# Attention's queries and keys written in two rounded parts by the scan, and its 66- and 67-row products filled up to 128 rows with zeros

## The chip, the cores and the metric

The kernel runs on one core of a Trainium2 chip. The metric is the time of one execution on the device in microseconds, as the median of several runs; a profile describes one further execution. The engines are called as the profile calls them: PE (TensorE, matrix products) with PEld (its weight loads), DVE (VectorE), ACT (ScalarE), POOL (GpSimd) and SP (SyncE, which here only issues transfers).

## What is computed

Two layers of a sequence model, 2048 tokens by 1024 features in float32. Each layer multiplies the normalised input by one wide matrix, gives the columns to four groups (forgetting attention, RWKV-7 time mixing, sliding-window attention, a short convolution), gates the results and multiplies them by an output matrix. The change touches the first group, four heads of width 64:

```python
q = _rmsnorm(q, q_norm)
k = _rmsnorm(k, k_norm)
log_f = jax.nn.log_sigmoid((f_logit + b_f).astype(jnp.float32))
Ft = jnp.cumsum(log_f, axis=1).transpose(0, 2, 1)
s = jnp.einsum("bqhd,bkhd->bhqk", qi, k) * scale
s = s + Fi[..., :, None] - Ft[:, :, None, :]
s = jnp.where(kpos[None, :] <= qpos[:, None], s, -jnp.inf)
p = jax.nn.softmax(s, axis=-1)
out = jnp.einsum("bhqk,bkhd->bqhd", p, v)
```

## The kernel before

A layer runs five stages one behind the other: `phase_project` and `phase_rwkv_prep` (0 to about 430 us in the first layer), `phase_rwkv_scan` (to about 1050), `phase_fox` (1054 to about 1337) and `phase_swa_out`. The second layer repeats them 1594.5 us later. Each engine has its own program, written by hand, and semaphores order them.

**The scan.** `phase_rwkv_scan` runs over 16 tiles `t` of 128 tokens, about 38 us each. PE interleaves the recurrence's small products with the input projection's dense ones, which are dealt out by `fill(stage)`; so PE has work at nearly every point, but its program is in order. Beside this, 56 units of 128 rows by 256 tokens are normalised: 32 are the queries and keys of `phase_fox` (`turned(u)` is false), 24 belong to the sliding window (true: they are also rotated, on POOL). A tile from `t = 4` on has four units, the outer two turned, the inner two plain. A unit goes: SP loads `qx` (L696); ACT squares it into `qr` (`square`, L1098); PE sums (`norm_sum`, L916); ACT makes the factor (L1105, L1107); POOL scales (`scale`, L814, and L824 for the last product) and raises `q_out`; SP stores it into `projT` (`store_norm`, L711). There are two `qr` buffers, so `square` of unit `u` waits until POOL has raised `q_out` for unit `u - 2`. In tiles 4 to 14 POOL computes, ahead of unit `(t, 1)`, the low part of the projection's next weights (L115) and the gates' bias (L829). `square(t, 3)` waits for unit `(t, 1)`, and PE's `norm_sum(t, 3)` waits for `square(t, 3)`.

**The attention.** `phase_fox` works in rounds `R`: pairs of heads `p` = 0 and 1, by blocks `Q` of 512 queries (8 rounds). Queries and keys are used as sums of two rounded parts (type fp32r), high and low. There are two sorts of score product. The `s` steps (L1510) compute scores from the high parts alone, `Q2` by `K2`, over 66 rows (64 and two rows of ones against the forget terms); DVE takes their maxima (`fx_nm`, L1599), from which the subtrahend of a round is made and put into rows 64 to 66 of `Q2` (steps `x` and `l`, L1519 on PE, L1663 on ACT). The `m` steps compute the scores that are used: `K1` by `Q1` (L1534, 128 rows) and `K2` by `Q2` over 67 rows (L1535); ACT takes the exponential (L1680), PE multiplies by the values (L1487), DVE and POOL add up the denominators (L1581, L1465). `plan()` writes the order of all steps by hand: the `s` steps of round R + 1 run between the `m` steps of round R. Steps `v` turn a block of values (L1497, copied by DVE at L1594).

`Q1` is the low part of q over its high part, `K1` the high part of k over its low part, `K2` and `Q2` the high parts in rows 0 to 63. Before, these come from raw q and k (SP, L1405 and L1406, 7 transfers a block with the forget terms, L1407, and the values, L1410) by steps `r`: ACT rounds (L1651, L1652, L1657), DVE subtracts (L1588, L1589), POOL copies (L1453), for each of 8 blocks a layer. At the start POOL writes ones into three rows of `Q2` (L1444), for which PE, ACT and the first block wait.

Of the kernel before, what the change touches and what calls it, by code (L numbers as in the profile page):

```python
# [13 lines left out]
F32 = mybir.dt.float32  # L14
# [571 lines left out]
def phase_rwkv_scan(nc, l, rw, pend, par, consts, masks, rope, fa, mixT, projT, J):  # L586
# [10 lines left out]
    with ExitStack() as ctx:  # L597
# [27 lines left out]
        cs = P.sb("cs", [128, 2, UB])  # L625
        qr = [P.sb(f"qr{e}", [128, UB]) for e in two]
# [15 lines left out]
        def turned(u):  # L642
            return norms[u][0] > 3

# [44 lines left out]
        def _(sp):  # L689

            def load_norm(u):
                e, (r, b) = u % 3, norms[u]
                row, cols = row_of[r], slice(PAD + b * UB, PAD + (b + 1) * UB)
                if u > 2:
                    sp.wait_ge(q_st[e], 16 * (u // 3))
# [12 lines left out]
            def store_norm(u):  # L708
                e, (r, b) = u % 3, norms[u]
                sp.wait_ge(s["q_out"], u + 1)  # L710
                sp.dma_start(projT[row_of[r]:row_of[r] + 128, PAD + b * UB:PAD + (b + 1) * UB], qx[e][:]).then_inc(q_st[e], 16)  # L711
# [90 lines left out]
            for q in range(3):  # L802
                sp.wait_ge(q_st[q], 16 * ((NU - q + 2) // 3))
# [4 lines left out]
        def _(pool):  # L808
            G = nc.gpsimd

            def scale(u):
# [447 lines left out]
def phase_fox(nc, l, projT, fa, consts, mixT, E):  # L1259
# [6 lines left out]
    with ExitStack() as ctx:  # L1266
# [9 lines left out]
        rq, rk, rv = [rows[0:HD, h] for h in two], [rows[0:HD, 2 + h] for h in two], rows[:, 4]  # L1276
        high, low = (w[:].rearrange("p k c -> p (k c)") for w in (E.wo_hi, E.wo_lo))
        Q1, K1 = ([[high[:, (i + h) * T:(i + h + 1) * T] for h in two], [P.sb(f"{n}1{h}", [128, T], F32R) for h in two]] for n, i in (("qa", 0), ("ka", 2)))
        Q2, K2 = ([[low[0:KX, (i + h) * T:(i + h + 1) * T] for h in two], [P.sb(f"{n}1{h}", [KX, T], F32R) for h in two]] for n, i in (("qb", 0), ("kb", 2)))
# [5 lines left out]
        LS = P.sb("LS", [128, QT, KX])  # L1285
        rl = P.sb("rl", [128, TB])
# [4 lines left out]
        names = ("c_in", "c_rdy", "a_split", "k_split", "d_split", "p_split", "s_rdy", "m_rdy", "x_rdy",  # L1291
                 "lt_rdy", "lt_free", "l_rdy", "v_rdy", "t_rdy", "p_rdy", "pv_done", "add_d", "add_p", "rl_rdy", "o_free", "rl_free", "yo_rdy", "whi_rdy", "wlo_rdy", "th_rdy", "gate_d")
        s = {n: P.sem(n) for n in names}
        raw_in, v_in, yo_st = ([P.sem(f"{n}{b}") for b in two] for n in ("raw_in", "v_in", "yo_st"))
# [12 lines left out]
        def plan():  # L1307
# [835 lines left out]
```

## Time and profile before

| | |
|---|---|
| median of 3 runs | 3163.36 us (3154.23 to 3169.47) |
| the profiled execution | 3179.65 us |
| its span, first to last instruction | 3177.8 us |
| PE busy in the span | 2972.4 us (94%) |
| DVE, ACT, POOL busy | 1468.2, 1133.4, 979.7 us |
| mean granted clock of PE | 0.946 of full speed |

The profiled execution is 16.3 us above the median of the runs, and 1.9 us of it lie outside the span. Sums over the trace are made against 3179.65. "PEclk" is the clock that PE was granted, as a share of full speed: 1.00 is 2.4 GHz, 0.50 is 1.2 GHz. PE's busy time counts a product that runs at the low clock with its longer duration, so a full PE can still be slow.

### The profile page before, as it was taken

To read this page: it belongs to the slowest core of one execution; us is meant where nothing else is said; L and a number is where in the kernel's file an instruction comes from. 1 tells how busy PE (TensorE), PEld (TensorE's weight loads), DVE (VectorE), ACT (ScalarE), POOL (GpSimd) and SP (SyncE) were. 2 spreads that over 40 slices of the span, in tenths; PEclk is the share of its full clock that TensorE was granted. 3 is DMA by queue.
4 is the path that set the end of the run, shared out by engine and by line. 5 is a ranking of instruction groups with operands and counts; after the bars stand their busy time and mean duration, and the time that the engine had idled before them with its cause. 6 is when DMAs were issued, how large, how long until landed. Compare 5 with 4: busy or idle time off the path is not lost. (4 is left out here: it accounts for less than half of the span.)

```text
span 3177.8 us, 67901 instructions
## 1 busy us (share of the span) xinstructions
PE 2972.4 (94%) x26644; PEld 2180.4 (69%) x26644; DVE 1468.2 (46%) x2204; ACT 1133.4 (36%) x2284; POOL 979.7 (31%) x890
## 2 busy tenths in 40 slices
PE   7999989999999789889889999899999997999799
PEld 6867867777777444367668678677777775444577
DVE  5127733322222577567451277333222224766674
ACT  5004433333333344633250044333333333446332
POOL 5101112344444224532141011123444442236221
PEclk9999999999999679989989999999999996799899
DMA  5224543344443211266332245434444432112663
GB/s 153 77 75 154 165 115 97 111 120 125 121 122 104 68 37 40 74 197 203 127 119 76 75 154 162 116 92 116 121 120 118 123 108 71 37 38 64 199 202 110
DMA packets 421183, 358.01 MB, mean 113 GB/s; under 512 B 127624, under 2 KB 358280, under 8 KB 420872
## 3 DMA queue, kind: packets, MB, share of 16 engines
q1 hardware_dynamic: 350696, 320.14, 33.5%
q10 hardware_dynamic: 70176, 33.59, 4.1%
q8 instruction: 211, 3.46, 0.5%
q14 instruction: 100, 0.82, 0.1%
HBM read 222.84 MB, written 130.84 MB: 111 GB/s over the span
## 5 line engine op out<-in xcount | busy, mean ns | idle before, releaser
L129 PE MATMUL ch_acc<-h_hi,ch_w_hi 128*128 128x512 f32 (+1 forms) x2048 | 822.7, 402 | 21.2 <-PEq L126 20.4
L135 PE MATMUL ch_acc<-h_hi,ch_w_lo 128*128 128x512 f32 (+1 forms) x2048 | 828.5, 405 | 0.0
L133 PE MATMUL ch_acc<-h_lo,ch_w_hi 128*128 128x512 f32 (+1 forms) x2048 | 825.8, 403 | 0.2 <-issue 0.2
L129 PEld LDWEIGHTS ch_acc<-h_hi,ch_w_hi 128*128 128x128 f32 (+1 forms) x2048 | 381.7, 186 | 108.5 <-issue 24.0
L133 PEld LDWEIGHTS ch_acc<-h_lo,ch_w_hi 128*128 128x128 f32 (+1 forms) x2048 | 381.5, 186 | 98.1 <-issue 11.5
L135 PEld LDWEIGHTS ch_acc<-h_hi,ch_w_lo 128*128 128x128 f32 (+1 forms) x2048 | 380.6, 186 | 89.1 <-issue 0.3
L115 POOL TENSOR_TENSOR ch_w_lo<-ch_raw,ch_w_hi 128x1024 fp32r<-128x1024 f32 (+1 forms) x62 | 149.1, 2404 | 744.8 <-POOLq L114 744.8
L1680 ACT ACTIVATE fx_prob<-fx_ST 128x512 f32<-128x512 f32 (+3 forms) x320 | 156.2, 530 | 201.1 <-PE fx_ST L1535 96.3
L1927 PE MATMUL so_acc<-ea_wo_hi,so_m_hi 128*128 128x512 f32 x512 | 207.4, 405 | 6.8 <-POOL so_m_lo L1862 6.8
L1929 PE MATMUL so_acc<-ea_wo_lo,so_m_hi 128*128 128x512 f32 x512 | 203.7, 398 | 0.0
L1599 DVE TENSOR_REDUCE fx_nm<-fx_SS 128x2 f32<-128x1024 f32 (+3 forms) x160 | 167.6, 1060 | 76.5 <-PE fx_SS L1510 63.8
L814 POOL TENSOR_SCALAR rs_qx<-rs_qx,rs_gain 128x256 f32<-128x256 f32 x112 | 103.4, 924 | 322.1 <-ACT rs_qr L1098 305.8
L1928 PE MATMUL so_acc<-ea_wo_hi,so_m_lo 128*128 128x512 f32 x512 | 202.4, 395 | 0.0
L1465 POOL TENSOR_TENSOR fx_sump<-fx_sump,fx_prob 128x1024 f32<-128x1024 f32 (+2 forms) x60 | 130.0, 2166 | 214.0 <-ACT fx_prob L1680 213.0
L146 ACT COPY ch_stage<-ch_acc 128x512 f32<-128x512 f32 x192 | 112.3, 585 | 225.9 <-ACTq L145 225.8
L146 DVE COPY ch_stage<-ch_acc 128x512 f32<-128x512 f32 (+1 forms) x64 | 44.1, 689 | 260.6 <-DVEq L145 260.6
L1862 POOL TENSOR_TENSOR so_m_lo<-so_y,so_m_hi 128x512 fp32r<-128x512 f32 x64 | 87.5, 1368 | 246.2 <-ACT so_m_hi L1805 241.2
L110 ACT ACTIVATE ch_w_hi<-ch_raw 128x1024 fp32r<-128x1024 f32 x64 | 65.9, 1029 | 243.3 <-ACTq L109 243.3
L824 POOL TENSOR_TENSOR rs_qx<-rs_qx,rs_qr 128x256 f32<-128x256 f32 x112 | 82.0, 732 | 143.9 <-ACT rs_qr L1107 132.8
L1581 DVE TENSOR_TENSOR fx_sumd<-fx_sumd,fx_prob 128x1024 f32<-128x1024 f32 (+3 forms) x72 | 117.5, 1632 | 10.6 <-ACT fx_prob L1680 3.6
L1927 PEld LDWEIGHTS so_acc<-ea_wo_hi,so_m_hi 128*128 128x128 f32 x512 | 96.8, 189 | 32.8 <-POOL so_m_lo L1862 7.3
L1929 PEld LDWEIGHTS so_acc<-ea_wo_lo,so_m_hi 128*128 128x128 f32 x512 | 96.5, 189 | 23.3
(285 smaller groups left out, 4932.1 us busy)
## 6 DMA issues: line engine op xcount, KB each, us to landing
projT<-ch_stage SPq DMA_DIRECT2D x248, 256.0 KB
ch_raw<-w_in ACTq DMA_DIRECT2D x62, 512.0 KB, 5.5
pj_xb<-x SPq DMA_DIRECT2D x32, 512.0 KB, 4.6
so_stage<-x SPq DMA_DIRECT2D x64, 256.0 KB, 3.4
rp_pre<-projT SPq DMA_DIRECT2D x16, 899.5 KB, 7.7
rs_qx<-projT SPq DMA_DIRECT2D x112, 128.0 KB, 3.3
projT<-rs_qx SPq DMA_DIRECT2D x112, 128.0 KB, 1.8
rs_cs<-rope SPq DMA_DIRECT2D x48, 256.0 KB, 3.7
```

Source lines behind the costliest of these rows:

```text
L115: (G or self.nc.gpsimd).tensor_tensor(self.w_lo[q][:, :, 0:m], self.raw[:, :, 0:m], self.w_hi[q][:, :, 0:m].bitcast(F32), ALU.subtract).th ...
L129: ins = M(acc, self.w_hi[q][:, k, 0:m], self.h_hi[:, k, cols], start=(k == 0), stop=False)
L133: M(acc, self.w_hi[q][:, k, 0:m], self.h_lo[:, k, cols], start=False, stop=False)
L135: ins = M(acc, self.w_lo[q][:, k, 0:m], self.h_hi[:, k, cols], start=False, stop=(k == KC - 1))
L146: copy(self.stage[e][0:m, :], self.acc[e][0:m, :]).then_inc(self.stage_rdy[e], 1)
L1465: G.tensor_tensor(sump[R % 2][:, :, lo:TB], sump[R % 2][:, :, lo:TB], prob[nt % NP][:, :, lo:TB], ALU.add).then_inc(s["add_p"], 1)
L1581: V.tensor_tensor(sumd[R % 2][:, :, lo:TB], sumd[R % 2][:, :, lo:TB], prob[i % NP][:, :, lo:TB], ALU.add).then_inc(s["add_d"], 1)
L1599: V.tensor_reduce(nm[p][:, :, t, c:c + 1], SS[ns % 2][:, :, 0:width(t, c)], AX.X, ALU.max, negate=True).then_inc(s["m_rdy"], 1)
L1680: A(prob[nt % NP][:, h, lo:TB], ST[h][:, lo:TB], ACT.Exp).then_inc(s["p_rdy"], 1)
L1927: M(a, m_hi[e][:, c, rows], wo_hi[:, c, cols], start=(i == 0), stop=False)
L1928: M(a, m_lo[e][:, c, rows], wo_hi[:, c, cols], start=False, stop=False)
L1929: ins = M(a, m_hi[e][:, c, rows], wo_lo[:, c, cols], start=False, stop=(i == KC - 1))
```

## The change

In the scan, POOL makes for each of the 32 plain units a layer both rounded parts: the last product is written once as fp32r into a new buffer `qh` and once into `x`, and `x` less `qh`, rounded, is the low part. SP stores both into a new tensor `qk` (two transfers for one). In `phase_fox` the steps `r` go; SP loads the parts straight into `Q1`, `K1`, `Q2`, `K2`, now 15 transfers a block. `Q2` and `K2` have 128 rows; POOL writes ones and zeros into rows 64 to 127 first, block 0 ahead of the rest, and SP waits for that. `s` and `m` products read all 128 rows. The constants are loaded from ACT's queue.

```diff
 def scale(u):                                  # POOL, scan
                 pool.drain()
                 pool.wait_ge(s["q_fac"], u + 1)
+                if not turned(u):
+                    f = plain.index(u)
+                    if f > 1:
+                        pool.wait_ge(q_st[plain[f - 2] % 3], stores[plain[f - 2]])
+                    G.tensor_tensor(qh[f % 2][:], x[:], qr[u % 2][:], ALU.mult)
                 G.tensor_tensor(x[:], x[:], qr[u % 2][:], ALU.mult)
+                if not turned(u):
+                    pool.drain()
+                    G.tensor_tensor(x[:].bitcast(F32R), x[:], qh[f % 2][:].bitcast(F32), ALU.subtract)
                 pool.drain().then_inc(s["q_out"], 1)
...
 def store_norm(u):                             # SP, scan
+                    for part, buf in ((0, qh[plain.index(u) % 2][:].bitcast(F32)), (1, qx[e][:])):
+                        row = (r // 2 * 2 + part) * GW + r % 2 * 128
+                        sp.dma_start(qk[row:row + 128, b * UB:(b + 1) * UB], buf).then_inc(q_st[e], 16)
...
-            beside = [("r", 0, i) for i in range(4)] + [("v", 0, 0)]
-            splits = [(R, [("r", B, i) for B in bs for i in range(4)]) for R, bs in ((0, (1,)), (1, (2,)), (2, (3, 4)), (3, (5, 6, 7)))]
-            splits = dict(splits)
+            beside = []
+            splits = {R: [("v", B, 0) for B in bs] for R, bs in ((0, (0, 1)), (1, (2,)), (2, (3, 4)), (3, (5, 6, 7)))}
...
 # SP, phase_fox, for each block R
+                sp.wait_ge(s["zero_rdy"], 1 if R == 0 else 2 if R < NQ else 3)
                 for h in two:
-                    sp.dma_start(rq[h][:, R % 2], projT[R_FQ + r:R_FQ + r + HD, tok]).then_inc(raw_in[R % 2], 16)
-                    sp.dma_start(rk[h][:, R % 2], projT[R_FK + r:R_FK + r + HD, tok]).then_inc(raw_in[R % 2], 16)
-                    sp.dma_start(K2[p][h][HD:KX, cols].bitcast(F32), fa[...]).then_inc(raw_in[R % 2], 16)
+                    sp.dma_start(Q2[p][h][0:HD, cols].bitcast(F32), qh[rows_of[h]]).then_inc(a_in[R], 16)
+                    sp.dma_start(K2[p][h][0:HD, cols].bitcast(F32), kh[rows_of[h]]).then_inc(a_in[R], 16)
+                    sp.dma_start(K2[p][h][HD:KX, cols].bitcast(F32), fa[...]).then_inc(a_in[R], 16)
+                for h in two:
+                    for buf, lo, hi in ((Q1[p][h], ql, qh), (K1[p][h], kh, kl)):
+                        sp.dma_start(buf[0:HD, cols].bitcast(F32), lo[rows_of[h]]).then_inc(b_in[R], 16)
+                        sp.dma_start(buf[HD:128, cols].bitcast(F32), hi[rows_of[h]]).then_inc(b_in[R], 16)
...
 # POOL, phase_fox
+            def filled(part, c, p, a, n):
                 for h in two:
-                    G.tensor_copy(Q2[p][h][HD:KX, :], LS[HD:KX, 0, 0:1].to_broadcast([KX - HD, T]))
-            pool.drain().then_inc(s["c_rdy"], 1)
+                    G.tensor_copy(part[p][h][HD:128, a:a + n], fill[HD:128, c:c + 1].to_broadcast([128 - HD, n]))
+                pool.drain().then_inc(s["one_rdy" if c == 0 else "zero_rdy"], 1)
+            filled(K2, 1, 0, 0, TB)
+            filled(Q2, 0, 0, 0, TB)
+            filled(K2, 1, 0, TB, T - TB)
+            filled(Q2, 0, 0, TB, T - TB)
+            filled(K2, 1, 1, 0, T)
+            filled(Q2, 0, 1, 0, T)
...
 # PE, phase_fox
-                        ins = M(SS[ns % 2][:, h, 0:w], Q2[p][h][0:HD + 2, t * 128:(t + 1) * 128], K2[p][h][0:HD + 2, c * TB:c * TB + w], start=True, stop=(c < Q))
+                        ins = M(SS[ns % 2][:, h, 0:w], Q2[p][h][:, t * 128:(t + 1) * 128], K2[p][h][:, c * TB:c * TB + w], start=True, stop=(c < Q))
...
-                if k == "r" and x > 1:                     # DVE
-                    V.tensor_tensor(Q1[p][h][0:HD, c], rq[h][:, R % 2], Q2[p][h][0:HD, c].bitcast(F32), ALU.subtract)
-                    ins = V.tensor_tensor(K1[p][h][HD:128, c], rk[h][:, R % 2], K2[p][h][0:HD, c].bitcast(F32), ALU.subtract)
...
-                if k == "r" and x < 2:                     # ACT; x == 2: two copies more, POOL: two copies
-                    A(Q2[p][x][0:HD, c], rq[x][:, R % 2], ACT.Copy)
-                    ins = A(K2[p][x][0:HD, c], rk[x][:, R % 2], ACT.Copy)
```

## Rows read from the trace of the kernel before

**Rows 1.** Page: PE busy tenths and granted clock tenths in 40 equal slices.

```profile
PE   7999989999999789889889999899999997999799
...
PEclk9999999999999679989989999999999996799899
```

**Rows 2.** Windows: the scan stage of the first layer.

```profile
430.00:1050.00 620.00, 611.14 (x9226) 467.26 (x9224) 183.40 (x389) 214.45 (x552) 243.35 (x306) 0.99 0.39 111
```

**Rows 3.** Windows in phase_fox: us, busy (x) per engine, PEclk, DMA share, GB/s.

```profile
1080.00:1190.00 110.00, 101.60 (x360) 55.22 (x359) 82.88 (x90) 49.20 (x96) 22.97 (x17) 0.70 0.12 35
1080.00:1112.00 32.00, 31.63 (x98) 18.39 (x97) 22.79 (x29) 14.89 (x29) 1.53 (x1) 0.50 0.09 26
1127.00:1146.00 19.00, 19.00 (x61) 11.25 (x61) 11.73 (x15) 8.08 (x17) 3.69 (x4) 0.50 0.14 43
...
1185.00:1330.00 145.00, 140.85 (x651) 68.80 (x649) 103.34 (x90) 82.76 (x149) 76.47 (x36) 1.00 0.19 54
2674.00:2796.00 122.00, 114.74 (x384) 62.60 (x383) 86.56 (x93) 52.65 (x102) 24.75 (x20) 0.66 0.10 31
2758.00:2764.00 6.00, 6.00 (x15) 2.57 (x15) 5.82 (x5) 3.15 (x6) 3.78 (x3) 0.50 0.00 0
```

**Rows 4.** Waits of PE over two microseconds, 1079 to 1190, then 2673 to 2796.

```profile
PE fx_SS L1510 <- DVE fx_nm L1599: 8.1, 5, 3.0
...
PE fx_SS L1510 <- DVE fx_nm L1599: 7.9, 5, 3.0
```

**Rows 5.** Groups by line on DVE, 1079 to 1190: busy us, mean ns, idle before.

```profile
L1588 DVE TENSOR_TENSOR fx_qa<-ea_rows,fx_qb 64x512 fp32r<-64x512 f32 x8 | 7.7, 960 | 0.0
...
L1589 DVE TENSOR_TENSOR ea_wo_hi<-ea_rows,ea_wo_lo 64x512 fp32r<-64x512 f32 x4 | 2.7, 684 | 0.1
```

**Rows 6.** Timeline of PE, one 128-row and one 67-row product.

```profile
1195.02 0.40 PE L1534 MATMUL fx_ST<-ea_wo_hi 128*128 128x512 f32 x1
1195.26 0.40 PE L1535 MATMUL fx_ST<-ea_wo_lo 67*128 67x512 f32 x1
```

**Rows 7.** Windows with PE alone, dense 128-row products after an idle start.

```profile
26.00:31.00 5.00, 5.00 (x19) 0.53 0.36 107
31.00:36.00 5.00, 5.00 (x30) 1.00 0.34 105
```

**Rows 8.** Timelines of POOL, SP and PE where phase_fox starts.

```profile
1054.57 3.75 POOL L1444 CAST ea_wo_lo<-fx_LS 3x2048 fp32r<-3x2048 f32 x2
...
1062.24 1.17 POOL L1453 CAST ea_wo_hi<-ea_rows 64x512 fp32r<-64x512 f32 x2 [0.25 <-issue]
...
1054.90 0.52 SPq L1405 DMA_DIRECT2D ea_rows<-projT  x1
...
1058.67 0.47 SPq L1405 DMA_DIRECT2D ea_rows<-projT  x1
...
1070.34 1.06 PE L1497 MATMUL fx_LT<-ea_ident,ea_rows 128*128 128x128 f32 x4
...
1075.73 1.12 PE L1519 MATMUL fx_LT<-ea_ident,fx_LS 128*67 128x128 f32 x4 [3.10 <-DVE fx_LS L1607]
```

**Rows 9.** Timelines in the scan, one tile: POOL, ACT, PE.

```profile
757.57 2.39 POOL L115 TENSOR_TENSOR ch_w_lo<-ch_raw,ch_w_hi 128x1024 fp32r<-128x1024 f32 x1 [4.46 <-POOLq L114]
760.19 0.60 POOL L829 TENSOR_SCALAR rs_ff<-rs_ff,rs_bf 4x128 f32<-4x128 f32 x1 [0.22 <-issue]
760.98 0.92 POOL L814 TENSOR_SCALAR rs_qx<-rs_qx,rs_gain 128x256 f32<-128x256 f32 x1 [0.20 <-issue]
762.06 0.73 POOL L824 TENSOR_TENSOR rs_qx<-rs_qx,rs_qr 128x256 f32<-128x256 f32 x1 [0.15 <-issue]
...
762.94 0.42 ACT L1098 ACTIVATE rs_qr<-rs_qx 128x256 f32<-128x256 f32 x1 [0.62 <-POOLq L825]
...
763.88 0.59 PE L916 MATMUL rs_bk<-rs_qr,rs_bones 128*128 128x256 f32 x2
```

More of the change, by code:

```diff
@@ L625, in phase_rwkv_scan @@
         cs = P.sb("cs", [128, 2, UB])
+        qh = [P.sb(f"qh{e}", [128, UB], F32R) for e in two]
         qr = [P.sb(f"qr{e}", [128, UB]) for e in two]
@@ L643, in turned @@
             return norms[u][0] > 3
+        plain = [u for u in range(NU) if not turned(u)]
+        stores = [sum(16 if turned(i) else 32 for i in range(u % 3, u + 1, 3)) for u in range(NU)]
         loads = [sum(96 if turned(i) else 16 for i in range(u % 3, u + 1, 3)) for u in range(NU)]
@@ L1275, in phase_fox @@
         rows = E.rows[:].rearrange("p k (e t) -> p k e t", e=2)
[L1276 removed]
+        rv = rows[:, 4]
         high, low = (w[:].rearrange("p k c -> p (k c)") for w in (E.wo_hi, E.wo_lo))
         Q1, K1 = ([[high[:, (i + h) * T:(i + h + 1) * T] for h in two], [P.sb(f"{n}1{h}", [128, T], F32R) for h in two]] for n, i in (("qa", 0), ("ka", 2)))
[L1279 removed]
+        Q2, K2 = ([[low[:, (i + h) * T:(i + h + 1) * T] for h in two], [P.sb(f"{n}1{h}", [128, T], F32R) for h in two]] for n, i in (("qb", 0), ("kb", 2)))
         vs = [E.vs0, P.sb("vs1", [128, NT, 128])]
@@ L1502, in _ @@
                     if x == 0:
-                        pe.wait_ge(s["a_split"], blocks[R])
-                        pe.wait_ge(raw_in[0], 96 * ((blocks[R] + 1) // 2))
-                        if blocks[R] > 1:
-                            pe.wait_ge(raw_in[1], 96 * (blocks[R] // 2))
+                        pe.wait_ge(s["one_rdy"], min(3, R + 1))
+                        for b in range(blocks[R]):
+                            pe.wait_ge(a_in[b], 96)
                     if ns > 1:
@@ L1524, in _ @@
                     if x == 0:
-                        pe.wait_ge(s["k_split"], blocks[R])
-                        pe.wait_ge(s["d_split"], blocks[R])
-                        pe.wait_ge(s["p_split"], blocks[R])
+                        for b in range(blocks[R]):
+                            pe.wait_ge(b_in[b], 128)
                         pe.wait_ge(s["l_rdy"], R + 1)
@@ L1644, in _ @@
             for k, R, x in order:
-                p, Q = divmod(R, NQ) if k in "rv" else rounds[R]
+                p, Q = divmod(R, NQ) if k == "v" else rounds[R]
                 c = slice(Q * TB, (Q + 1) * TB)
-                if k == "r" and x < 2:
-                    act.wait_ge(raw_in[R % 2], 96 * (R // 2 + 1))
-                    if R == 0:
-                        act.wait_ge(s["c_rdy"], 2)
-                    A(Q2[p][x][0:HD, c], rq[x][:, R % 2], ACT.Copy)
-                    ins = A(K2[p][x][0:HD, c], rk[x][:, R % 2], ACT.Copy)
-                    if x == 1:
-                        act.drain().then_inc(s["a_split"], 1)
-                if k == "r" and x == 2:
-                    for h in two:
-                        ins = A(K1[p][h][0:HD, c], rk[h][:, R % 2], ACT.Copy)
-                    ins.then_inc(s["k_split"], 1)
                 if k == "l":
```

67 lines of the change are left out of this document (29 added, 38 removed).

## The prediction

> **What bounds the kernel now.** I read the page's slices first. PE is busy in 7 to 9 tenths of nearly every slice, so it is the bound; but its granted clock falls to 6 or 7 tenths in two places, and these are the first halves of `phase_fox` in the two layers [rows 1]. Then windows by stage. In the scan PE is busy for 611.1 of 620 us at a clock of 0.99 [rows 2]: whatever makes PE wait there is paid in full, since nothing is left to hide it. In `phase_fox` the windows split in two. From 1185 to 1330 PE is full at clock 1.00. From 1080 to 1190 (and 2674 to 2796) it is busy for 101.6 of 110 us (114.7 of 122), at clocks of 0.70 and 0.66 [rows 3]. As there are two levels, 1.2 and 2.4 GHz, a mean of 0.70 means 2 x 0.30 x 110 = 66 us at the lower level, and 0.66 means 83 us. The reader should see two things in these windows: PE was full through 1080 to 1112 and through 1127 to 1146 and still had the lower clock, while the same kinds of product kept 1.00 once it was granted, through 145 us. Last the waits: the only wait of weight in these two stretches is PE's `s` step waiting for DVE's maxima, 8.1 and 7.9 us [rows 4]. These are the pauses behind which the clock falls again.
>
> How much work lies in the two stretches at the full clock: PE's busy time less half of the time at the low clock, 101.6 - 33 = 68.6 us, and 114.7 - 41.5 = 73.2 us. DVE is busy there for 82.9 and 86.6 us [rows 3], next behind PE, and so the engine that stands in the way once PE is fast.
>
> **The change part by part.**
>
> *Steps `r` go.* On DVE they are 24 subtractions in the stretch 1079 to 1190 (blocks 2 to 7): 16 of 0.96 and 8 of 0.68 us [rows 5], 20.8 us. DVE keeps 62 us of work in the first layer's stretch and 66 in the second's: less than PE's 68.6 and 73.2. ACT loses six roundings or copies of 64 rows a block, and POOL two of 0.58 us each (1.17 for two [rows 8]); neither bounds PE, so I cost them at nothing. The waits of 8.1 and 7.9 us [rows 4] should mostly go, since DVE was late there behind its subtractions. I keep 5 us a layer for what remains (DVE is within 7 us of PE, and the two are not even at each moment); bounds 0 and 8.
>
> *Rows of zeros.* A product over 67 rows takes the same time as one over 128: both 0.40 us at the full clock for 512 columns [rows 6]. The filling costs PE nothing itself. What it does to the clock no row of before shows directly. The nearest rows: dense 128-row products after an idle start got the full clock within 5 us [rows 7]; the attention's mix, in which four of ten products have 66 or 67 rows, stood at the low one for 32 us in one stretch and 19 in another, and for little more than 6 us in a third, where all products were 512 columns wide [rows 3]. So the mix gets the clock late and unevenly where the dense case got it soon, and filling four of ten products up makes it more like the dense case. Bounds: no effect, with the first 32 us of each stretch at the low clock as before, or 5 us as in the dense case. I take 10 us: the steps of round 0 are narrow, and the values' products and the masks are not changed. Later falls of the clock came behind PE's waits for DVE, and I take them to go with these waits.
>
> So the first stretch becomes 10 us at the low clock (5 us of the work), 63.6 us of the rest, and 5 us of waits: 79 us in place of 110. The second: 10 + 68.2 + 5 = 83 in place of 122. **Gain 31 + 39 = 70 us.** The part from 1185 on is full at clock 1.00 and gains nothing.
>
> *The start of `phase_fox`.* SP now waits until POOL has filled block 0 of `K2`. POOL writes one of 2048 columns in 1.9 us (3.75 for two) and one of 512 in 0.6 [rows 8]; SP starts its loads at about 1056.3 in place of 1054.9. It issues 7 transfers in 3.77 us [rows 8], 0.54 each, so 15 take 8.1 us a block. The block of values of block 1 is issued 30th: 1056.3 + 16.2 = 1072.5, landed at about 1074.5. `plan()` puts `v` of block 1 ahead of the last `s` step of round 0, so this step is late: PE turned that block at 1070.3 before, and would now at 1074.6. Round 0's subtrahend was turned at 1075.7 [rows 8], at that time behind DVE's subtractions; now it would be some 3.5 us behind the values (one `s` step, a reduction, `x`), 1078. In exchange, ACT's and POOL's part is shorter. I take **1.5 us later a layer, 3 in all**; bounds for both layers -3 (the earlier start of the first scores wins) and +8. Behind that, SP is ahead: seven blocks more at 8.1 us end near 1121 if it never waits, and the scores that need all blocks started at 1180 and will start at about 1150. It costs nothing there; the cover is 30 us.
>
> *The scan.* This is where the change pays. POOL gets a second product and a subtraction for each of 32 plain units a layer. One such instruction takes 0.73 us, and 0.15 us lie between two with a drain [rows 9]: 0.73 + 0.15 + 0.73 = 1.61 us later for `q_out`. As POOL is busy for 243 of 620 us [rows 2], this looks free; but look at who waits. In tiles 4 to 14, L115, L829, L814 and L824 run on POOL nearly without a gap, from 757.57 to 762.79; ACT's `square(t, 3)` has waited 0.62 us for this (L825) and starts at 762.94; it ends at 763.36, and PE's L916 comes at 763.88 [rows 9]. PE is 0.5 us from waiting. The same spacing stands in 20 of the 22 tiles of this kind (11 a layer); in the other two PE comes 0.5 and 0.9 us later. So 1.61 - 0.5 = 1.1 us of wait a tile: 20 x 1.1 + 0.6 + 0.2 = 23 us. PE's program is in order, and its dense products stand behind L916. Everything later in the tile (factor, gates, DVE's scan of them) moves with PE and was not tight: the gates' logarithms on ACT wait behind `square(t, 3)`, but DVE's use of them lies 4 us behind. In tiles 0 to 3 and 15, where POOL starts sooner or `square` comes 5.6 us ahead of PE, nothing is lost. SP's second store of a unit adds 0.4 us behind `q_out`; queued behind it are the projection's next store and the load of a later unit, both with over 1.5 us to spare. Bounds: 0 (if rounding overlaps more than I think) and 22 x 1.6 = 35. **23 us lost.**
>
> *The sum*: -70 + 3 + 23 = -44 us, against the profiled 3179.65: 3135.6. The profiled execution stood 16.3 us over the median; I take the difference to the median: 3163.4 - 44 = **3119 us**.
>
> **The rivals.**
>
> *A. The scan's price is hidden*: the units' new work finds room after all. For it: POOL is 60% idle. Against it: the chain of rows 9. -70 + 3 = -67: 3096 us.
>
> *B. Zero rows don't count*: the clock rises no sooner, and only the falls behind DVE's waits go. 32 us at the low clock (16 us of the work) + 52.6 + 3 = 88 us in the first layer, 32 + 57.2 + 3 = 92 in the second: gain 22 + 30 = 52; -52 + 26 = -26: 3137 us. For it: 6 us were once enough for the mix [rows 3]; against it: twice, 19 us and more of a full PE were not. The Trainium skill ("TensorE: Matmul & The Clock Gate", "HAM oscillation — how this bites in real kernels") asks only that PE have no idle gaps, and says nothing of rows; by that rule this rival is the result. It does not explain the 32 us, in which PE was full.
>
> *C. The clock goes on as before.* With the full clock PE outruns DVE (62 against 68.6 us of work, unevenly spread), pauses, and loses it again. With all 149 us at the low clock kept, the stretches are 68.6 + 33 and 73.2 + 41.5, so only the pauses are gained, 8.4 + 7.3 = 16; -16 + 26 = +10: 3173 us.
>
> *D. Slower*: as C, but PE has the low clock for longer than before, because its pauses in the first rounds are now cut by DVE at full pace and by loads of SP. Each 2 us more at the low clock cost 1 us. The sum is zero at 128 us at the low clock in the two stretches together, and the kernel is slower by over 0.5% from 160 us on; with 180 us it is +26: 3189 us.
>
> **How the numbers follow.** A measurement of this kernel can tell about 0.5%, 16 us, from no change. Forecast 0.48, A 0.08, B 0.18, C 0.14, D 0.12. B lies with most of its width beyond 16 us. Faster: the forecast, A and 0.16 of B, 0.72; within 0.5%: the rest of B, 0.02, and C, 0.16; slower: D, 0.12. The range takes in A below and C above: 3093 to 3175. It leaves out D and the far side of A, under 0.2. The forecast's own range, from its bounds (gain 60 to 75, scan 15 to 30, start -3 to +8), is 3100 to 3141.
>
> **What would show it.** (1) PEclk in the first 120 us of `phase_fox`: near 0.95 in place of 0.70 and 0.66; under 0.8 is B or C. (2) L1588, L1589, L1651 to L1657 gone, DVE about 21 us lighter, PE's waits for `fx_nm` under 5 us a layer. (3) In the scan a new wait of PE at L916 (or its weight load) for L1098, some 1.1 us in 20 to 22 tiles; the stage 11 to 12 us longer a layer. If there is none, the step on rows 9 is wrong. (4) The second `v` of `phase_fox` at 20 us from its start in place of 16. (5) The stage from 1185 on unchanged in length. The prediction fails if SP issues its transfers at over 0.8 us each, so that loads and not PE set the first half, or if POOL's two new instructions are slower than 0.73 us.

## The result and the profile after

The changed kernel takes 3140.45 us (median of 6 runs, 3137.85 to 3142.7) against 3160.8 us of the kernel before in the same comparison (6 runs, 3154.23 to 3169.47): ratio 0.9942, 95% interval 0.9922 to 0.9962, 20 us or 0.6% faster. Forecast were 44 us, to 3119 us. The measured time lies at the edge of the forecast's own range (3100 to 3141) and nearer to rival B's 3137 than to the forecast: the total alone can't tell the two apart, the clock in the profile and the run without the rows of zeros do. The profiled execution took 3140.46 us, with a span of 3138.7, a granted clock of 0.968 (0.946 before) and DVE busy for 1419.2 us (1468.2 before). Line numbers have moved: the `s` product is L1529 (was L1510), its maxima L1610 (L1599), the `m` products L1552 and L1553 (L1534, L1535), `v` L1517 (L1497), `x` L1538 (L1519), and in the scan `square` L1116 (L1098), `norm_sum` L934 (L916).

Page of the kernel after, PE's busy share and granted clock in tenths (as rows 1):

```profile
PE   7999989999999699879979999899999996998899
PEclk9999999999999799989989999999999998999899
```

Windows of the kernel after: the scan (as rows 2), then in `phase_fox` the stretches of rows 3, shifted by 14 us in the first layer and by -12 in the second, and the 4 us before and behind the rise of the clock. The columns are those of rows 3.

```profile
430.00:1064.00 634.00, 615.22 (x9228) 467.67 (x9227) 182.97 (x389) 214.49 (x552) 291.69 (x370) 0.99 0.41 116
...
1094.00:1204.00 110.00, 101.11 (x471) 54.40 (x472) 85.94 (x84) 41.17 (x82) 24.62 (x14) 0.95 0.34 102
1094.00:1126.00 32.00, 28.23 (x133) 17.01 (x133) 23.37 (x30) 9.71 (x20) 1.04 (x1) 0.84 0.68 202
...
2662.00:2784.00 122.00, 112.90 (x516) 60.08 (x514) 96.67 (x90) 45.26 (x90) 29.13 (x16) 0.95 0.31 94
...
1100.00:1104.00 4.00, 4.00 (x13) 2.58 (x14) 1.26 (x3) 1.19 (x2) 0.00 (x0) 0.50 0.66 195
1104.00:1108.00 4.00, 3.42 (x16) 1.76 (x15) 3.86 (x5) 0.00 (x0) 0.00 (x0) 0.99 0.77 222
```

The clock in these stretches is 0.95 in place of 0.70 and 0.66, and PE finishes 471 and 516 instructions in place of 360 and 384. The full clock comes at 1104, 3.3 us behind the first `m` step (4.5 us in the second layer), and doesn't fall again before 1329, 8 us ahead of the stage's end. DMA moves 202 GB/s in the first 32 us, where it moved 26.

Waits of PE in the kernel after, first the stretch 1094 to 1204 (as rows 4), then the scan of the first layer, then the start of `phase_fox`, 1066 to 1104:

```profile
PE fx_SS L1529 <- DVE fx_nm L1610: 6.6, 6, 1.5
...
PE rs_bk L934 <- ACT rs_qr L1116: 11.1, 11, 1.3
...
PE fx_LT L1517 <- DMA ea_rows<-projT: 12.9, 2, 7.6
PE fx_SS L1529 <- DMA ea_wo_lo<-fa: 11.9, 1, 11.9
```

The second line is the wait that the prediction placed in the scan: eleven times a layer, just over 1 us. Timelines of the tile of rows 9 after the change, POOL, ACT and PE:

```profile
764.11 2.39 POOL L115 TENSOR_TENSOR ch_w_lo<-ch_raw,ch_w_hi 128x1024 fp32r<-128x1024 f32 x1 [4.46 <-POOLq L114]
...
768.65 0.73 POOL L838 TENSOR_TENSOR rs_qh<-rs_qx,rs_qr 128x256 fp32r<-128x256 f32 x1 [0.21 <-issue]
769.34 0.74 POOL L839 TENSOR_TENSOR rs_qx<-rs_qx,rs_qr 128x256 f32<-128x256 f32 x1
770.23 0.73 POOL L842 TENSOR_TENSOR rs_qx<-rs_qx,rs_qh 128x256 fp32r<-128x256 f32 x1
...
771.10 0.42 ACT L1116 ACTIVATE rs_qr<-rs_qx 128x256 f32<-128x256 f32 x1 [2.24 <-POOLq L843]
...
771.57 0.70 PE L934 MATMUL rs_bk<-rs_qr,rs_bones 128*128 128x256 f32 x2 [0.99 <-ACT rs_qr L1116]
```

From the start of L115 to `square` it is 6.99 us; before it was 762.94 - 757.57 = 5.37 [rows 9]. The difference, 1.62 us, is the 1.61 of the forecast.

Start of `phase_fox`, which begins at 1068.22 (as rows 8): SP issues the values of blocks 0 and 1, PE turns them, then the first subtrahend and the first `m` product:

```profile
1078.71 0.59 SPq L1426 DMA_DIRECT2D ea_rows<-projT  x1
1087.87 0.37 SPq L1426 DMA_DIRECT2D ea_rows<-projT  x1
...
1082.73 1.12 PE L1517 MATMUL fx_LT<-ea_ident,ea_rows 128*128 128x128 f32 x4 [5.27 <-DMA ea_rows<-projT]
...
1092.44 1.11 PE L1517 MATMUL fx_LT<-ea_ident,ea_rows 128*128 128x128 f32 x4 [7.59 <-DMA ea_rows<-projT]
...
1096.43 1.12 PE L1538 MATMUL fx_LT<-ea_ident,fx_LS 128*67 128x128 f32 x4 [1.65 <-DVE fx_LS L1618]
...
1100.74 0.63 PE L1552 MATMUL fx_ST<-ea_wo_hi 128*128 128x512 f32 x1
```

The first `m` step is at 32.5 us from the start of the stage in the first layer and at 32.9 in the second, where it was at 26.0 in both.

Between the two profiled executions the time goes as follows. The end of `phase_fox` is taken as DVE's first instruction of the last stage (1347.2 before in the first layer, not the 1337 given for the kernel before; 1337.1 after). The second layer's projection and preparation are taken up to the start of its scan.

| part, both layers together | forecast | measured |
|---|---|---|
| scan | +23 | +13.1 + 9.6 = +22.7 |
| `phase_fox` up to the first `m` step | +3 | +6.5 + 6.9 = +13.4 |
| `phase_fox` behind it | -70 | -30.9 - 36.2 = -67.1 |
| second layer's projection and preparation | 0 | -8.7 |
| the rest | 0 | +0.5 |
| sum | -44 | -39.2 |

The profiled execution before took 3179.65 us, 18.9 above the median of this comparison; the one after lay on its median. So -39.2 + 18.9 = -20.3 us, the measured difference. Two things were off: the start of `phase_fox`, and what the profiled execution before stands for.

### The profile page after: what moved, and what is told of

Its sections match the earlier page's. It is cut to its first block and busy times, and to the rows that moved or that the text cites. A ratio compares the mean times of both kernels' runs of the same rounds, so it can differ in the third digit from the quotient of the medians.

```text
span 3138.7 us, 68173 instructions
## 1 busy us (share of the span) xinstructions
PE 2905.0 (93%) x26644; PEld 2137.8 (68%) x26644; DVE 1419.2 (45%) x2140; ACT 1080.8 (34%) x2188; POOL 1071.7 (34%) x1006
## 5 line engine op out<-in xcount | busy, mean ns | idle before, releaser
L129 PEld LDWEIGHTS ch_acc<-h_hi,ch_w_hi 128*128 128x128 f32 (+1 forms) x2048 | 380.4, 186 | 108.2 <-issue 24.2
L133 PEld LDWEIGHTS ch_acc<-h_lo,ch_w_hi 128*128 128x128 f32 (+1 forms) x2048 | 380.1, 186 | 96.4 <-issue 10.2
L115 POOL TENSOR_TENSOR ch_w_lo<-ch_raw,ch_w_hi 128x1024 fp32r<-128x1024 f32 (+1 forms) x62 | 150.2, 2422 | 732.0 <-POOLq L114 732.0
L1610 DVE TENSOR_REDUCE fx_nm<-fx_SS 128x2 f32<-128x1024 f32 (+3 forms) x160 | 166.5, 1059 | 58.2 <-PE fx_SS L1529 35.6
L1599 DVE TENSOR_TENSOR fx_sumd<-fx_sumd,fx_prob 128x1024 f32<-128x1024 f32 (+3 forms) x72 | 125.5, 1743 | 10.8 <-ACT fx_prob L1681 3.6
L1928 PEld LDWEIGHTS so_acc<-ea_wo_hi,so_m_hi 128*128 128x128 f32 x512 | 96.9, 189 | 32.8 <-POOL so_m_lo L1863 7.3
L1929 PEld LDWEIGHTS so_acc<-ea_wo_hi,so_m_lo 128*128 128x128 f32 x512 | 96.9, 189 | 22.1
```

The lines of the kernel that those rows point to most:

```text
L115: (G or self.nc.gpsimd).tensor_tensor(self.w_lo[q][:, :, 0:m], self.raw[:, :, 0:m], self.w_hi[q][:, :, 0:m].bitcast(F32), ALU.subtract).th ...
L129: ins = M(acc, self.w_hi[q][:, k, 0:m], self.h_hi[:, k, cols], start=(k == 0), stop=False)
L133: M(acc, self.w_hi[q][:, k, 0:m], self.h_lo[:, k, cols], start=False, stop=False)
L1599: V.tensor_tensor(sumd[R % 2][:, :, lo:TB], sumd[R % 2][:, :, lo:TB], prob[i % NP][:, :, lo:TB], ALU.add).then_inc(s["add_d"], 1)
L1610: V.tensor_reduce(nm[p][:, :, t, c:c + 1], SS[ns % 2][:, :, 0:width(t, c)], AX.X, ALU.max, negate=True).then_inc(s["m_rdy"], 1)
L1928: M(a, m_hi[e][:, c, rows], wo_hi[:, c, cols], start=(i == 0), stop=False)
```

## The experiments

Each run below was timed beside the kernel before, whose median there was 3156.9 to 3161.8 us, but not beside the kernel after (3140.45 us, with 3160.8 for the kernel before). So a difference against the kernel after is good to about 4 us.

### The kernel before once more

No edit; one further profiled execution, to see what the 3179.65 us execution had of its own.

> The kernel before, unchanged, for a second trace. The prediction was a difference against one execution of 3179.65 us, 16 to 19 us over the median of its runs. Theory: these 19 us lie where the clock is uncertain: in the second layer's projection (232.4 us in the trace before, 224.5 in the first layer) and in the attention stages (293.2 and 299.0 us). Then this trace shows an attention stage of 285 to 293 us in each layer and a second projection near 224 us, and the changed kernel saved less there than the first trace suggested. Rival: the 19 us are spread evenly over all stages, as for a clock of another rate; then each stage is shorter by 0.6% and no more.

It took 3155.1 us, 24.5 less. Windows of this execution in `phase_fox` of both layers (as rows 3; the second layer begins 20 us sooner), then the second layer's projection, for the first profiled execution of the kernel before and for this one:

```profile
1080.00:1190.00 110.00, 101.83 (x381) 55.31 (x380) 84.59 (x93) 51.75 (x101) 25.58 (x19) 0.74 0.12 35
2654.00:2776.00 122.00, 113.65 (x411) 61.11 (x410) 87.51 (x95) 55.16 (x107) 25.78 (x21) 0.72 0.11 32
```

```profile
1584.00:1814.00 230.00, 206.66 (x915) 160.95 (x916) 62.80 (x68) 51.44 (x90) 53.49 (x23) 0.91 0.29 93
```

```profile
1584.00:1814.00 230.00, 212.59 (x975) 165.31 (x974) 71.66 (x88) 52.45 (x90) 55.05 (x23) 0.96 0.29 92
```

The clock stood at 0.74 and 0.72 in place of 0.70 and 0.66, and `phase_fox` took 581.5 us in both layers together in place of 592.2: 10.7 of the 24.5 us. 14.9 lie between the two `phase_fox`, of which 9 in the second layer's projection and preparation, with a clock of 0.96 in place of 0.91 in the window shown. The excess isn't spread evenly, so the rival falls. The time for which PE has the low clock differs between executions of one kernel, and 10.7 us of the gain against the first execution are not a gain against this one.

### The change without the rows of zeros

```diff
-  M(SS..., Q2[p][h][:, t * 128:(t + 1) * 128], K2[p][h][:, c * TB:c * TB + w], ...)
+  M(SS..., Q2[p][h][0:HD + 2, t * 128:(t + 1) * 128], K2[p][h][0:HD + 2, c * TB:c * TB + w], ...)
-  M(o, K2[p][h][:, a], Q2[p][h][:, b], ...)
+  M(o, K2[p][h][0:KX, a], Q2[p][h][0:KX, b], ...)
```

> The changed kernel with its score products over 66 and 67 rows again (the rows of zeros are written and not read); loads, scan and all else as changed. Theory (rows count for the clock): the stretch from the first m step to the end of round 3's scores, 77.6 us at a clock near 1.00 in the changed kernel, falls to the low clock for 20 to 32 us at its start and becomes 10 to 16 us longer a layer; the whole 3160 to 3172 us. Rival B (only DVE's waits mattered, rows do not count): clock and time as in the changed kernel, 3140 us plus or minus 4.

3179.31 us (median of 6, 3161.49 to 3182.84), ratio to before 1.0067 (1.0046 to 1.0087): without the zeros the change is a loss, and 39 us slower by the medians than with them. Windows of its first `phase_fox`; the first `m` step is at 1099.45:

```profile
1106.00:1110.00 4.00, 3.82 (x12) 2.33 (x11) 3.74 (x6) 0.08 (x1) 0.00 (x0) 0.50 0.73 211
1110.00:1130.00 20.00, 20.00 (x63) 11.09 (x62) 9.57 (x12) 6.28 (x13) 0.66 (x1) 0.50 0.42 134
1130.00:1134.00 4.00, 4.00 (x22) 2.29 (x22) 2.73 (x3) 1.08 (x2) 0.38 (x1) 0.96 0.23 66
```

PE is full for 20 us without a pause and has the low clock throughout; the clock rises 31 us behind the first `m` step, against 3.3 with zeros. The edit changes nothing but the rows that are read, so this settles rival B's question, and it falls: the zeros decide. The time is 7 us above what the theory allowed.

The profile was of the fastest run, and in profiles only 21 us lie between the two kernels. So a further execution of the same kernel was profiled:

> The kernel e1_rows_66_67 once more, for one look: its six runs stood between 3161 and 3183 us, and its profile was of the 3161 us run. Theory (the slower ones lose time in phase_fox, as the profiled execution before: the lower clock for 30 us behind the first products, and again behind pauses): an execution of about 3180 us shows a clock below 0.8 in windows of phase_fox that have 0.95 to 1.00 in the profile at 3161. Rival (they lose it elsewhere: projection or last stage): phase_fox of 279 to 281 us in both layers as in the first profile.

This execution took 3177.19 us, 15.7 more than the first. `phase_fox` took 280.7 us in the first layer (280.4 in the other execution) and 292.1 in the second (278.8). Windows of the second layer, first of the execution of 3161 us, then of this one; their first `m` steps are at 2680.80 and 2685.16:

```profile
2694.00:2714.00 20.00, 20.00 (x106) 11.53 (x108) 15.38 (x16) 8.98 (x19) 3.40 (x2) 1.00 0.56 174
2724.00:2741.00 17.00, 17.00 (x47) 8.20 (x48) 5.62 (x7) 5.51 (x11) 1.76 (x2) 0.51 0.20 64
```

```profile
2696.00:2716.00 20.00, 20.00 (x63) 10.96 (x61) 9.28 (x12) 5.99 (x13) 0.94 (x1) 0.50 0.45 140
2737.00:2753.00 16.00, 16.00 (x42) 7.68 (x40) 5.20 (x6) 5.01 (x10) 1.76 (x2) 0.50 0.21 64
2778.00:2784.00 6.00, 6.00 (x19) 3.54 (x18) 4.16 (x3) 0.77 (x2) 1.63 (x1) 0.50 0.00 0
```

Both executions lose the full clock once for 17 us with PE full. What differs, as the theory had it, is that the clock rises 31 us behind the first `m` step in place of 13, and that it falls once more, for 7 us: 25 us more at the low clock, which cost about half of that, 12.5 of the stage's 13.3 us (an estimate). So of the 39 us, 21 stand in the profile of the fastest run already, and a later rise and a further fall of the clock account for most of what this slower execution adds. The six times of the kernel after lie within 5 us, and its profile shows no such fall. Its waits are no shorter, though. Ahead of the 49th and the 55th `s` product of a layer PE waits 1.4 to 1.5 us and then 1.0 us in both kernels; behind this pair the clock fell in the second layer of both executions with 66 and 67 rows, and in neither layer with 128.

### The rows of zeros alone

Everything as before, but `Q2` and `K2` have 128 rows, POOL fills them, SP waits for block 0, and the products read all rows. The steps `r` and the scan are those of before.

```diff
+  sp.wait_ge(s["zero_rdy"], 1 if R == 0 else 2 if R < NQ else 3)
-  M(SS..., Q2[p][h][0:HD + 2, t * 128:(t + 1) * 128], K2[p][h][0:HD + 2, c * TB:c * TB + w], ...)
+  M(SS..., Q2[p][h][:, t * 128:(t + 1) * 128], K2[p][h][:, c * TB:c * TB + w], ...)
```

> The kernel before with one part of the change: rows 64 to 127 filled and all 128 rows read by the score products; raw queries and keys are loaded and split in the attention as before, and the scan is as before. Theory: the full clock comes within 10 us of the first m step, although DVE still has its 21 us of subtractions; DVE's waits of 8 us a layer stay and may bring the clock down again. 12 to 22 us less a layer: 3117 to 3137 us, so faster than the whole change. Rival B: no change to before, 3160 plus or minus 8 us, with 60 us and more at the low clock in each layer.

3143.97 us (3139.84 to 3144.74), ratio 0.9954 (0.9938 to 0.997): slower than the theory's 3117 to 3137, and faster than rival B's 3160 plus or minus 8. Waits of PE for the maxima over the whole execution, this kernel and then the second execution of before:

```profile
PE fx_SS L1525 <- DVE fx_nm L1614: 40.1, 23, 7.0
```

```profile
PE fx_SS L1510 <- DVE fx_nm L1599: 21.4, 13, 3.0
```

The clock is full 2.5 us behind the first `m` step (5.1 in the second layer), and then PE waits for DVE, which still has the subtractions: 40 us where the kernel after waits for 13, and the clock is back at 0.83 in the window from 62 to 82 us of the first layer's stage. The first `m` step also comes later than before, at 30.1 us from the start of the stage in both layers. So the two halves of the change need one another. Against the 3156.9 us of before in this comparison, the zeros alone gain 13 us, and the moved rounding alone loses 22; both together gain 20. Without the scan's price of 25 us (next run) the moved rounding alone would take about 3179.3 - 25.4 = 3153.9 us, 3 less than before (an estimate; it wasn't tried), and both together take 42 less than before, which the next run shows.

### The scan's buffer freed behind the product

```diff
+  G.tensor_tensor(x[:], x[:], qr[u % 2][:], ALU.mult).then_inc(s["q_mul"], 1)
   if not turned(u):
...
-      G.tensor_tensor(qh[f % 2][:], x[:], qr[u % 2][:], ALU.mult)
-  G.tensor_tensor(x[:], x[:], qr[u % 2][:], ALU.mult)
-  if not turned(u):
+      pool.drain()
+      G.tensor_copy(qh[f % 2][:], x[:])
       pool.drain()
       G.tensor_tensor(x[:].bitcast(F32R), x[:], qh[f % 2][:].bitcast(F32), ALU.subtract)
...
-  act.wait_ge(s["q_out"], u - 1)          # square
+  act.wait_ge(s["q_mul"], u - 1)
```

> The changed kernel, but in the scan POOL multiplies first and tells ACT at once that the factor's buffer is free; the rounded copy and the subtraction come behind. The result is the same and POOL has no less work. Theory: the 22 waits of PE at the norm's sum, 21.5 us in all, go, and the time is 3140 - 21 = 3119 us (3115 to 3123). Rival: POOL's added work costs by its amount (3.3 us a tile), or through SP's second store; then the waits move to another line of the scan and the time stays within 5 us of 3140.

3115.01 us (3112.68 to 3116.06), ratio 0.9868 (0.9849 to 0.9887), 25 us less than the kernel after and at the lower edge of the theory's range. Timelines of POOL, ACT and PE in the tile of rows 9:

```profile
763.21 0.73 POOL L834 TENSOR_TENSOR rs_qx<-rs_qx,rs_qr 128x256 f32<-128x256 f32 x1 [0.15 <-issue]
764.10 0.40 POOL L840 CAST rs_qh<-rs_qx 128x256 fp32r<-128x256 f32 x1 [0.15 <-issue]
...
764.04 0.42 ACT L1116 ACTIVATE rs_qr<-rs_qx 128x256 f32<-128x256 f32 x1 [0.57 <-POOL rs_qx L834]
...
765.02 0.59 PE L934 MATMUL rs_bk<-rs_qr,rs_bones 128*128 128x256 f32 x2
```

`square` starts as soon as the product is done, beside the rounding, and PE no longer waits. The wait of 21.5 us (22 times) over both layers has gone from the list, so the scan's price was this buffer and not POOL's work as such: POOL does nearly the same work here (a copy of 0.40 us in place of a second product of 0.73).

### The start of `phase_fox`: which queue, which order

`second_parts(eng, R)` stands for the eight loads of `Q1` and `K1` of a block. First, those of blocks 0 and 1 moved to ACT's queue:

```diff
-  (SP, each block: second parts ahead of the values)
+  if R > 1: second_parts(sp, R)
...
+  for R in two: second_parts(act, R)      # ACT, behind the two constants
```

> The kernel after, but in phase_fox ACT's queue issues the second parts (Q1 and K1, 8 transfers a block) of blocks 0 and 1, so that SP issues for these blocks only the first parts, the forget terms and the values: the values of block 1 are SP's 14th transfer in place of its 30th. In the kernel after, PE waits at the start of phase_fox 6.2 us a layer for the terms of block 0 (common to both theories) and 7.6 us for the values of block 1, and the first m step comes 32.5 to 32.9 us after the start of the stage. My theory (the start of phase_fox is late because these values stand behind 29 other transfers of SP, at 0.60 us each): the first m step comes at 22 to 27 us, the rest of the stage keeps its length, and the kernel takes 3122 to 3133 us, 8 to 18 less than the kernel after. Rival (the loads are limited by what the DMA engines move, about 200 GB/s in this window, not by SP's issues): the first m step moves by under 2 us, 3137 to 3141 us.

3134.97 us (3133.49 to 3136.11), 5.5 less than the kernel after, where I expected 8 to 18. The first `m` step came at 29.0 us, between the theory's 22 to 27 and the rival's over 30.5. SP's issue of block 1's values, PE's step, and the median time from issue to landing of the values (last number), here and then in the kernel after:

```profile
1077.35 0.43 SPq L1434 DMA_DIRECT2D ea_rows<-projT  x1
...
1087.57 1.12 PE L1525 MATMUL fx_LT<-ea_ident,ea_rows 128*128 128x128 f32 x4 [5.11 <-DMA ea_rows<-projT]
...
ea_rows<-projT SPq DMA_DIRECT2D x5, 256.0 KB, 10.1
```

```profile
ea_rows<-projT SPq DMA_DIRECT2D x4, 256.0 KB, 4.1
```

Issued 9.2 us sooner, turned by PE 3.5 us sooner: of the gain in issuing, nearly 6 us went into a longer landing (10.2 us for this load, 4.5 in the kernel after). The first scores came 3.6 to 4.5 us later, while their loads shared the engines with the second parts. The Trainium skill ("DMA: Bandwidth & Descriptors", "Issuing engines are not separate DMA queues") says this: transfers started by several engines end on the same 16 DMA engines, and a second engine saves only the time that it takes to start them. The trace agrees, with the 9.2 us saved in issuing and the 5.7 us lost in landing.

Next, SP's order alone: first parts and values of blocks 0 and 1, then the second parts of both.

```diff
+  if R > 1: second_parts(sp, R)
...
   sp.dma_start(rv[:, R % 2], ...)
+  if R == 1:
+      second_parts(sp, 0)
+      second_parts(sp, 1)
```

> The kernel after, but SP issues for blocks 0 and 1 of phase_fox first the parts that the s steps need and the values (14 transfers), and then the second parts of both blocks (16 transfers); ACT's queue issues none of them. In e5_values_first the values of block 1 were issued at 10.5 us from the start of the stage, in place of 19.7, but took 10.1 us to land, in place of 4.1, and the first scores came 3.6 to 4.5 us later than in the kernel after: with two queues the same DMA engines were full. Theory (two limits at nearly the same place: SP's issues at 0.6 us each, and what the DMA engines move; only the order gains more): the first s step stays at 7.4 us, the values of block 1 are turned at 15 to 17 us in place of 24.2, the first m step comes at 22 to 25 us in place of 32.5, and the kernel takes 3120 to 3128 us. Rival (something else holds the first m step at about 28 us as in e5_values_first, as the landing of the second parts of block 0): 3133 to 3137 us.

The first `m` step came at 21.5 us, 11 sooner than in the kernel after. But the kernel took 3135.48 us (3133.04 to 3138.05), only 5 less. PE in this kernel:

```profile
1081.94 1.12 PE L1528 MATMUL fx_LT<-ea_ident,ea_rows 128*128 128x128 f32 x4 [1.87 <-DMA ea_rows<-projT]
...
1102.19 1.11 PE L1528 MATMUL fx_LT<-ea_ident,ea_rows 128*128 128x128 f32 x4 [6.93 <-DMA ea_rows<-projT]
```

The values of block 2 are still the 45th transfer, and PE now waits for them for 6.9 us. In this wait the clock falls, and it stays low for 10 us, in 6 of which PE works:

```profile
1094.80:1098.20 3.40, 0.46 (x4) 0.23 (x3) 1.71 (x2) 0.00 (x0) 0.00 (x0) 0.99 0.74 196
1098.20:1108.40 10.20, 6.02 (x20) 4.03 (x20) 4.79 (x7) 0.49 (x1) 0.00 (x0) 0.50 0.75 207
```

At 8.9 us a block the loads set the pace up to round 2, and a better order only moves the wait. The time is the rival's, but not its reason: theory and rival both took the first `m` step for the measure of the gain, which it isn't.

### Both edits together, and the best version

> The kernel after with both edits: in the scan POOL frees the factor's buffer right behind its first product (as in e4_free_after_product), and ACT's queue issues the second parts of blocks 0 and 1 of phase_fox (as in e5_values_first). The two lie in different stages, so if each cause is its own, the gains add: the 3115.0 us of e4_free_after_product less what e5_values_first gains against the kernel after, which I expect to be 8 to 18 us: 3097 to 3107. Rival (the start of phase_fox only moves the wait to DVE or to the clock): 3113 to 3117 us.

3108.75 us (3104.93 to 3110.65), ratio 0.9836 (0.9818 to 0.9854).

> The kernel after with the edit of e4_free_after_product in the scan and the order of e7_values_14th at the start of phase_fox. Theory: 3115 less 12 to 20, 3095 to 3103 us. Rival of e7_values_14th: 3108 to 3112 us, as e6_both.

3108.86 us (3106.28 to 3112.24), ratio 0.985 (0.9826 to 0.9874). Both miss their theories (3097 to 3107, 3095 to 3103). Each is 6 us below the kernel with the freed buffer alone: the two causes add, and the start gives the 5 to 6 us that it gave alone. For the last version the second parts of block 0 are on ACT's queue, behind the landing of block 0's values, so that they don't compete with the first loads, and SP is eight issues ahead for block 2:

```diff
+  act.wait_ge(v_in[0], 16)
+  second_parts(act, 0)
...
+  if R == 1: second_parts(sp, 1)          # SP
```

> e4_free_after_product, with the first parts and the values of blocks 0 and 1 of phase_fox issued first on SP's queue (as in e7_values_14th), the second parts of block 0 on ACT's queue once the values of block 0 have landed, and those of block 1 next on SP's. In e7_values_14th the first m step came 11 us sooner, but the values of block 2, still SP's 45th transfer, were late for it: PE waited 6.9 us for them. Theory (the loads of blocks 0 to 2 as a whole set the pace until round 2, by SP's issues more than by bytes): SP is 8 issues or 4.8 us ahead for block 2, the first m step comes at 20 to 23 us, the wait for the values of block 2 falls under 3 us, the stage takes 262 to 264 us, and the kernel 3098 to 3106 us. Rival (the DMA engines' bytes set it, 1.8 MB a block at about 200 GB/s, 9 us): the wait for block 2 stays at 5 us or more, 3107 to 3113 us, as e8_e4_and_e7.

3101.65 us (3098.91 to 3106.28), ratio 0.9823 (0.9799 to 0.9846): 7 us less than the two above, 39 less than the kernel after. PE's waits for values over both layers:

```profile
PE fx_LT L1527 <- DMA ea_rows<-projT: 12.6, 4, 4.3
```

It was 18.9 in the kernel with SP's order alone. These sums hold the waits for the values of blocks 1 and 2. `phase_fox` took 264.2 and 261.3 us, where it took 268.9 and 269.7 after the change. The time is the theory's, though the first `m` step came at 23.9 and 23.7 us, a little behind its 20 to 23. The wait for block 2 was 3.4 us in the first layer, between the theory's 3 and the rival's 5, and 0.9 in the second: issues count for most of it, not for all. The clock fell in the wait of 3.4 us, for 6.8 us, and not in the one of 0.9; the second layer's stage is 2.9 us shorter.

### Which products need the rows

`m` products over 128 rows and `s` products over 66, then the other way round; each is one of the two edits of the run without rows of zeros.

> The kernel after, but the s products (one of the two sorts) read 66 rows as before; the m products read 128. e1_rows_66_67, with 66 and 67 rows in both, took 3179.3 us, the kernel after 3140.5. Theory (each sort counts by its share of PE's work: in the first half of a layer's phase_fox the s steps take the larger part of the filled products, 2.5 s steps for one m step in rounds 0 and 1): most of the 39 us is lost, 3158 to 3175 us, with the clock at the lower level for 20 to 30 us behind the start of the products. Rival (only that no product of the dense m steps is left with 67 rows matters): 3140 to 3148 us.

> The kernel after, but the m products (K2 by Q2) read 67 rows as before; the s products read 128. Theory (each sort counts by its share of PE's work): the smaller part is lost, 3141 to 3155 us, and the sum of what this run and e9_m_rows_128 lose is about the 39 us of e1_rows_66_67. Rival (the m products decide): 3165 to 3180 us.

With 66 rows in `s`: 3154.89 us (median of 10, 3142.41 to 3172.8). With 67 rows in `m` alone: 3144.03 us (median of 10, 3141.68 to 3146.5). The first lies between its theory (3158 to 3175) and the rival (3140 to 3148). The second lies in its theory's range, but the sum that this theory forecast fails: the losses, 14.4 and 3.6 us, add up to 18 and not to the 39 of both. The 3.6 us are within the 4 us that this comparison leaves open. Windows of the first, then of the second; their first `m` steps are at 1098.00 and 1100.29:

```profile
1110.00:1114.00 4.00, 4.00 (x16) 2.37 (x12) 1.56 (x2) 0.34 (x1) 0.00 (x0) 0.50 0.58 181
1114.00:1130.00 16.00, 16.00 (x78) 8.47 (x77) 10.66 (x13) 8.01 (x17) 1.04 (x1) 0.95 0.47 139
```

```profile
1104.00:1108.00 4.00, 4.00 (x15) 2.57 (x13) 3.58 (x5) 0.00 (x0) 0.00 (x0) 0.53 0.76 237
1108.00:1112.00 4.00, 3.48 (x19) 1.93 (x18) 3.71 (x6) 0.98 (x2) 0.00 (x0) 1.00 0.57 175
```

| products with 66 or 67 rows | first `m` step to full clock, layer 1, layer 2 | spread of the times |
|---|---|---|
| `s` and `m` (kernel before, first and second execution) | 32.6, 32.2 and 13.7, 32.8 us | 15 us (6 runs) |
| `s` and `m` (loads and scan as after, first and second execution) | 30.9, 12.8 and 30.5, 31.0 us | 21 us (6 runs) |
| `s` | 17.7, 21.8 us | 30 us (10 runs) |
| `m` | 7.4, 8.5 us | 5 us (10 runs) |
| neither (kernel after) | 3.3, 4.5 us | 5 us (6 runs) |
| neither (rows of zeros alone) | 2.5, 5.1 us | 5 us (6 runs) |

## Why the prediction was right and wrong

*The bound.* Right: the low clock in the first half of `phase_fox` was the time to win, and the part behind it did not move (from the subtrahend of round 4 to the end of `phase_fox`, in the first layer, 117.4 us before and 116.5 after).

*Rows of zeros and the steps `r`.* Right in mechanism and, against the same execution, near in size: 67.1 us of the forecast 70. The low clock behind the first `m` step lasted 3.3 and 4.5 us where I took 10. DVE became lighter by 24.5 us a layer. Its waits are 6.6 and 6.7 us in the two stretches, not under 5, but the longest is 1.5 us in place of 3.0, and the clock doesn't fall behind them. Part of the nearness is luck: with the measured low clock and waits the same working gives about 73 us (an estimate), so it overstates by 6 us, and the errors in these two inputs hid half of that. What I did not see is that neither half alone gives its share.

*The scan.* Right: 22.7 for 23 us, a wait of 1.0 us on average, at most 1.3, at `norm_sum` in 22 tiles, 21.5 us in all. The chain of rows 9 was read to its end, from the queue ahead on POOL to the engine that runs in order, and the run with the freed buffer shows that this buffer was the cause.

*The start of `phase_fox`.* The step that failed in size: 6.5 and 6.9 us a layer for 1.5, and outside the bound of 8 for both. The values of block 1 were issued 19.7 us from the start of the stage, where the sum gives 17.9, since 9 or 10 of the 15 transfers take 0.60 us each and a block 8.9, not 8.1: the 0.54 us was the mean of the old mix, in which two of seven take 0.60. They took 4.5 us to land where I took 2 and the kernel before took 2.8; the queue in front of them was fuller, with 191 GB/s over the first 40 us of the stage in place of 94. That this made the landing longer is argued; the run with a second queue, where the same load took 10.2 us, fits it. So `v` of block 1 came at 24.2 us, not at 20, and the first `m` step behind it at 32.5, not at 27.5. My test for it (issues over 0.8 us each) was too lax: it asked when the loads would set the whole first half, and not when they would set the first round. "Behind that, SP is ahead" held only because the first round was late: the runs on the order of the loads found block 2 late as soon as that round was faster.

*From the execution to the median.* The second step that failed, with about the same effect (18.9 - 8.2 = 10.7 us against 10.4). I took the whole difference, worked out on an execution 16.3 us above the median, from the median. But part of what made that execution slow was the low clock in `phase_fox` itself: 10.7 us of the gain was already missing from a faster execution. Another part lay in the second layer's projection and preparation, which the change doesn't touch, and vanished by itself: -8.7 us. One further execution of the kernel before stands behind this, so the split of the excess is known for these two executions and not for the median. With the errors of the three terms, the change elsewhere, and the excess over the median, which is not in the kernel after: -44 + 10.4 + 2.9 - 0.3 - 8.2 + 18.9 = -20.3.

*The rivals.* A falls (the scan's price was paid in full). B falls (39 us), although the total came within 4 us of its 3137: its mechanism is not what happened. C and D fall: the clock was kept. The Trainium skill's rule that I weighed for B, that PE must have no idle gaps ("TensorE: Matmul & The Clock Gate", "HAM oscillation — how this bites in real kernels"), doesn't cover this: PE was full for 20 us at the low clock with 66 and 67 rows, and got the full clock 3.3 and 4.5 us behind the first `m` step with 128.

## What to carry to other kernels

Where a full PE keeps the low clock, look at how many rows its products read: filling them up with zeros costs it nothing (both 0.40 us [rows 6]) and here brought 13 us alone and 39 with the rest of the change. When a change multiplies transfers, follow them to the second and third block and price landing in a full queue, not in an empty one. And before a difference worked out on one execution is taken from a median, ask which stages made that execution slow; if it is the stage that you are changing, the excess is part of your gain and not of the median's. Last, release a buffer behind its last reader, not at the end of the work that follows: that was worth more here (25 us) than the change itself (20).

## What the runs showed of the hardware

In these kernels the granted clock depended on the rows that the products read, and not on PE's busy time alone. With 66 and 67 rows in 21 of the 62 products that start in the window 1110 to 1130, PE stayed at 1.2 GHz through 20 us without a pause, and had 2.4 GHz 13 to 33 us behind the first `m` step. With 128 rows in both sorts it had it after 2 to 5 us, in both layers of all eight such kernels. Filling only one of the two sorts lay between (7 to 9 us with the `s` products filled, 18 to 22 with the `m` products). With 128 rows in the `s` products the times of each kernel also lay within 3 to 8 us, and with fewer within 12 to 30. What exactly the chip looks at these runs don't show.

The clock fell in PE's waits of 6.9 us and 3.4 us for the values of block 2, for 10 and 7 us, and not behind one of 0.9 us.

A transfer of 64 rows took SP 0.45 us or 0.60 us to issue. Two queues at once raised the rate in about the first 40 us of `phase_fox` from about 190 to 226 GB/s, and the median landing of a 256 KB transfer from 4.1 to 10.1 us.
